# Four groups of head probabilities turned by transfer instead of on TensorE, and the last eight mixer blocks in a new order

## The reference, cut to what matters

```python
def hybrid_mixer(h, mem, positions, ...):
    proj = h @ w_in                       # q, k, v of moba and fox, pool input, memory q, 4 x 1024 gates
    o_a = from_heads(moba_attention(q_a, k_a, v_a))          # 8 heads of 64, causal over 256 rows
    o_b = multiscale_pool(pool_u, pool_mix, pool_scale)
    o_c = from_heads(forgetting_attention(q_c, k_c, v_c, log_f))   # 8 heads of 64, causal, decaying
    o_m = memory_cross_attention(mem_q, mem, ...)            # 4 heads of 128
    branches = jnp.stack([o_a, o_b, o_c, o_m], axis=2)
    y = jnp.einsum('bsnc,ncd->bsnd', branches, w_branch)
    gates = jax.nn.sigmoid(gate_logits.reshape(b, s, N_BRANCH, D_MODEL))
    return jnp.sum(gates * y, axis=2) @ w_out

def softmax_times_values(logits, v):      # the core of each attention
    p = jax.nn.softmax(logits, axis=-1)
    return jnp.einsum('bhqk,bhkd->bhqd', p, v)
```

## Time and profile before

| | |
|---|---|
| median of 3 runs | 1324.23 us (1324.18 to 1324.59) |
| the profiled execution | 1324.54 us, of which its span is 1322.70 us |
| PE busy | 1317.1 us of the span, 6092 matmuls |
| PE's weight loads / DVE / ACT / POOL busy | 1088.3 / 933.0 / 689.6 / 293.1 us |
| granted TensorE clock | 1.00 over the run |
| the chain that ended last | PE 99% |
| in the stretch 334 to 385 us (steps 59 to 66 or so, layer 0) | PE 51.00 of 51 us, DVE 50.13, ACT 30.75, POOL 23.75 |
| in 385 to 436 us | PE 51.00 of 51 us, DVE 38.56, ACT 30.55, POOL 4.19 |

### The profile page before, as it was taken

The page is one execution under the profiler, slowest core; times in us unless marked ns, Lnnn a source line. Parts: engine busy times, 40 slices in busy tenths (PEclk is TensorE's granted clock), DMA queues, the critical chain, the costliest instruction groups (busy, mean ns, idle before and its releaser), DMA issues.

```text
span 1322.7 us, 15761 instructions
## 1 busy us (share of the span) xinstructions
PE 1317.1 (100%) x6092; PEld 1088.3 (82%) x6092; DVE 933.0 (71%) x1174; ACT 689.6 (52%) x956; POOL 293.1 (22%) x280
## 2 busy tenths in 40 slices
PE   9999999999999999999999999999999999999999
PEld 7888888888888888888888888888888878888887
DVE  6666777789987675665475664787999876665653
ACT  5444465554756455444455454556556554645442
POOL 0324312033431002323003230020524110023220
PEclk9999999999999999999999999999999999999999
DMA  9877566567666447777557775555767665577671
GB/s 320 257 216 223 173 230 202 192 179 265 201 178 212 161 149 248 204 225 215 191 191 223 210 228 192 194 165 177 221 223 199 207 195 179 173 225 222 208 215 64
DMA packets 205354, 269.48 MB, mean 204 GB/s; under 512 B 94160, under 2 KB 103904, under 8 KB 205280
## 3 DMA queue, kind: packets, MB, share of 16 engines
q1 hardware_dynamic: 204096, 265.24, 64.9%
q0 software_dynamic: 896, 3.16, 0.7%
q10 hardware_dynamic: 288, 0.07, 0.0%
HBM read 245.37 MB, written 1.06 MB: 186 GB/s over the span
## 4 chain that ended last, share of the span: by engine, by line
PE 99%; DMA 0%; DVE 0%; issue 0%; ACT 0%; SPq 0%; DVEq 0%; ACTq 0%
PE psum L699 24%; PE psum L962 23%; PE psum L726 21%; PE psum L707 12%; PE psum L967 12%; PE psum L920 1%; PE psum L820 1%; PE psum L858 1%; PE psum L924 1%; PE psum L867 1%; PE psum L825 1%; PE psum L654 0%; PE psum L836 0%; PE psum L905 0%; PE psum L861 0%; PE psum L805 0%
## 5 line engine op out<-in xcount | busy, mean ns | idle before, releaser
L1452 DVE TENSOR_TENSOR ring_lo<-raw,ring_hi 128x1024 fp32r<-128x1024 f32 x459 | 598.7, 1318 | 317.1 <-ACT ring_hi L1033 315.5
L1033 ACT ACTIVATE ring_hi<-raw 128x1024 fp32r<-128x1024 f32 x463 | 481.5, 1048 | 555.8 <-PE psum L707 235.5
L699 PE MATMUL psum<-ring_hi,hT 128*128 128x512 f32 x1408 | 348.1, 389 | 1.0 <-DVE ring_hi L1896 1.0
L699 PEld LDWEIGHTS psum<-ring_hi,hT 128*128 128x128 f32 x1408 | 264.2, 188 | 56.0 <-DVE ring_hi L1896 1.2
L962 PE MATMUL psum<-ring_hi,hT 128*128 128x512 f32 x960 | 240.1, 392 | 0.0
L962 PEld LDWEIGHTS psum<-ring_hi,hT 128*128 128x128 f32 x960 | 178.4, 188 | 38.4 <-issue 1.0
L707 PE MATMUL psum<-ring_lo,hT 128*128 128x512 f32 x704 | 188.4, 389 | 0.0
L1340 POOL COPY planes<-gate 128x1024 uint16<-128x1024 uint16 (+1 forms) x48 | 69.0, 1465 | 455.8 <-DVE gate L1526 455.8
L707 PEld LDWEIGHTS psum<-ring_lo,hT 128*128 128x128 f32 x704 | 131.9, 188 | 27.2
L967 PE MATMUL psum<-ring_lo,hT 128*128 128x512 f32 x480 | 128.3, 389 | 0.0
L1350 POOL COPY prodT<-planes_T 128x512 uint16<-128x512 uint16 (+1 forms) x96 | 87.4, 977 | 104.4 <-DMA planes_T<-planes 104.4
(11 more groups left out here) (196 smaller groups left out, 1199.7 us busy)
## 6 DMA issues: line engine op xcount, KB each, us to landing
raw<-in_w_ffn_in SPq DMA_DIRECT2D x78, 1024.0 KB, 5.3
raw<-in_w_in SPq DMA_DIRECT2D x64, 1024.0 KB, 5.5
raw<-in_w_ffn_out SPq DMA_DIRECT2D x44, 1024.0 KB, 5.0
raw<-in_w_branch SPq DMA_DIRECT2D x16, 1024.0 KB, 5.6
raw<-in_w_ffn_in SPq DMA_DIRECT2D x19, 512.0 KB, 4.9
raw<-in_w_mem_kv SPq DMA_DIRECT2D x8, 1024.0 KB, 5.1
raw<-in_w_out SPq DMA_DIRECT2D x8, 1024.0 KB, 5.0
forget<-negc_rows POOLq DMA_DIRECT2D x2, 1024.0 KB, 8.3
```

The source lines that it names most:

```text
L699: pe.matmul(outs[t][:, :], hT[part][:, kc, t * P:(t + 1) * P], w[0][:, kc - first, :], start=kc == 0 and part == 0, stop=False)
L1033: act.activation(unit_out(0, step, k), view, ACT.Copy).then_inc(hi_done.sem, 1)
L1452: dve.tensor_tensor(unit_out(1, step, k), view, unit_out(0, step, k).bitcast(F32), ALU.subtract)\
```

## The change

Groups 3 and 5 join groups 2 and 4: all four head groups are turned by planes, and the PE way (`BY_PE`, the `probsT` stage, its three semaphores) is gone. Group 3's planes are written by ACT at step 63, its transfers are behind the load of step 69 (second home: the memory branch's `vals`), and its `values` move from step 64 END to step 68 MIDDLE. Group 5's planes are written at step 73, its transfers are behind the load of step 78, and its `values` move from step 74 MIDDLE to step 76 MIDDLE. In both branches the blocks come as gate, gate, y, y: after the change the steps are 67/68 gate (0,0), 69/70 gate (0,1), 71 y (0,0), 72 y (0,1), 73/74 gate (2,0), 75/76 gate (2,1), 77 y (2,0), 78 y (2,1). Group 5's scores move from step 71 to step 70 and its exps from 72 to 71. The turn of the first half of z moves from the end of step 77 to the middle of step 78, and DVE adds y (2,0) before the remainder of step 79's second unit.

```diff
     for n in (0, 2):
         for dh in range(2):
             block("gate", (n, dh))
+        for dh in range(2):
             block("y", (n, dh), 1)
...
-_plan("zT", 0, _step_of("gate", (2, 1), 1))
+_plan("zT", 0, _step_of("y", (2, 1)), pe=MIDDLE, act=MIDDLE, dve=START)
...
-BY_DMA, BY_PLANES, BY_PE = (0, 1), (2, 4), (3, 5)
-PLANES_BEHIND = {_step_of("y", (3, 1)): 2, _step_of("gate", (2, 0), 1): 4}
+BY_DMA, BY_PLANES = (0, 1), (2, 3, 4, 5)
+PLANES_BEHIND = {_step_of("y", (3, 1)): 2, _step_of("gate", (0, 1)): 3, _step_of("gate", (2, 0), 1): 4, _step_of("y", (2, 1)): 5}
...
-    (3, _step_of("kc", None, 1), _step_of("gate", (3, 1)), _step_of("gate", (3, 1), 1), _step_of("y", (3, 1))),
-    (4, _step_of("gate", (0, 0)), _step_of("gate", (0, 0), 1), None, _step_of("y", (0, 1))),
-    (5, _step_of("gate", (0, 1), 1), _step_of("y", (0, 1)), _step_of("gate", (2, 0)), _step_of("gate", (2, 0), 1)),
+    (3, _step_of("kc", None, 1), _step_of("gate", (3, 1)), _step_of("gate", (3, 1), 1), _step_of("gate", (0, 0), 1)),
+    (4, _step_of("gate", (0, 0)), _step_of("gate", (0, 0), 1), _step_of("gate", (0, 1)), _step_of("y", (0, 1))),
+    (5, _step_of("gate", (0, 1), 1), _step_of("y", (0, 0)), _step_of("gate", (2, 0)), _step_of("gate", (2, 1), 1)),
...
-                elif stage == "probsT":
-                    pe.wait_ge(probs_ready.sem, probs_ready.at(L, arg + 1))
-                    for j in range(2):
-                        for odd in range(2):
...
-                merged(L, 4)
+                for g in BY_PLANES[1:]:
+                    merged(L, g)
...
+                    summing = (kind, arg) == ("y", (2, 0))
+                    if summing:
+                        serve(L, MIX0 + i, kind, arg, half)
                     ahead(L, MIX0 + i, 1)
                     tasks(L, i, EARLY)
-                    serve(L, MIX0 + i, kind, arg, half, (lambda: lo(L, MIX0 + i + 3, 0)) if kind == "qa" else None)
+                    if not summing:
+                        serve(L, MIX0 + i, kind, arg, half, (lambda: lo(L, MIX0 + i + 3, 0)) if kind == "qa" else None)
```

More of the change, by code:

```diff
@@ L161 @@
     TASKS.setdefault(("DVE", _step_of("vc"), (MIDDLE, EARLY)[t]), []).append(("causal", t))
-_plan("zT", 0, _step_of("gate", (2, 1), 1))
+_plan("zT", 0, _step_of("y", (2, 1)), pe=MIDDLE, act=MIDDLE, dve=START)
 _plan("zT", 1, _step_of("out", 0))
-BY_DMA, BY_PLANES, BY_PE = (0, 1), (2, 4), (3, 5)
-PLANES_BEHIND = {_step_of("y", (3, 1)): 2, _step_of("gate", (2, 0), 1): 4}
+BY_DMA, BY_PLANES = (0, 1), (2, 3, 4, 5)
+PLANES_BEHIND = {_step_of("y", (3, 1)): 2, _step_of("gate", (0, 1)): 3, _step_of("gate", (2, 0), 1): 4, _step_of("y", (2, 1)): 5}
 TURNED_BEHIND = dict(zip([_step_of("ka"), _step_of("gate", (3, 0), 1)], BY_DMA))
-for g, scores, exps, turned, summed in [
+for g, scores, exps, planes, summed in [
     (0, _step_of("y", (1, 0)), _step_of("qa"), None, _step_of("gate", (1, 1), 1)),
     (1, _step_of("gate", (1, 1), 1), _step_of("y", (1, 1)), None, _step_of("qc")),
-    (2, _step_of("gate", (3, 0)), _step_of("gate", (3, 0), 1), None, _step_of("gate", (3, 1), 1)),
-    (3, _step_of("kc", None, 1), _step_of("gate", (3, 1)), _step_of("gate", (3, 1), 1), _step_of("y", (3, 1))),
-    (4, _step_of("gate", (0, 0)), _step_of("gate", (0, 0), 1), None, _step_of("y", (0, 1))),
-    (5, _step_of("gate", (0, 1), 1), _step_of("y", (0, 1)), _step_of("gate", (2, 0)), _step_of("gate", (2, 0), 1)),
+    (2, _step_of("gate", (3, 0)), _step_of("gate", (3, 0), 1), _step_of("y", (3, 0)), _step_of("gate", (3, 1), 1)),
+    (3, _step_of("kc", None, 1), _step_of("gate", (3, 1)), _step_of("gate", (3, 1), 1), _step_of("gate", (0, 0), 1)),
+    (4, _step_of("gate", (0, 0)), _step_of("gate", (0, 0), 1), _step_of("gate", (0, 1)), _step_of("y", (0, 1))),
+    (5, _step_of("gate", (0, 1), 1), _step_of("y", (0, 0)), _step_of("gate", (2, 0)), _step_of("gate", (2, 1), 1)),
 ]:
@@ L181 @@
     if g in BY_PLANES:
[L182 to L185, removed]
+        TASKS.setdefault(("ACT", planes, EARLY), []).append(("planes", g))
+    _plan("values", g, summed, pe=MIDDLE if g in (2, 3, 5) else END, act=MIDDLE if g == 2 else START if g == 5 else EARLY,
           dve=START if g in (1, 2, 5) else EARLY)
@@ L362, in build @@
         head_merged = tally("head_merged", len(BY_PLANES))
-        pT_ps = tally("pT_ps", len(BY_PE))
-        pT_act = tally("pT_act", len(BY_PE))
-        pT_dve = tally("pT_dve", len(BY_PE))
         pv_ready = tally("pv_ready", 6)
@@ L433, in planes_out @@
         def planes_out(g):
-            homes = [kmem[:, :, :], qkT_buf[:, FOX % 2, 1]] if g // 2 == MOBA else [qkT_buf[:, MOBA % 2, i] for i in range(2)]
+            homes = [kmem[:, :, :], vals[:, MEM] if g % 2 else qkT_buf[:, FOX % 2, 1]] if g // 2 == MOBA else [qkT_buf[:, MOBA % 2, i] for i in range(2)]
             return [words.rearrange("p t c -> p (t c)")[:, 0:768].bitcast(U16) for words in homes]
@@ L811, in task @@
                     if arg >= 2:
-                        attended(L, arg - 1 if arg - 1 in BY_PLANES else arg)
+                        attended(L, max(2, arg - 1))
                     if arg:
@@ L841, in task @@
                         pe.wait_ge(pT_merged.sem, pT_merged.at(L, BY_DMA.index(arg) + 1))
-                    elif arg in BY_PLANES:
+                    else:
                         pe.wait_ge(head_merged.sem, head_merged.at(L, BY_PLANES.index(arg) + 1))
[L844 to L847, removed]
+                        pe.wait_ge(max_ready.sem, max_ready.at(L, min(arg + 2, 6)))
                     if arg:
@@ L1217, in task @@
                     last.then_inc(head_planes.sem, 1)
-                elif stage == "probsT":
-                    act.wait_ge(pT_ps.sem, pT_ps.at(L, BY_PE.index(arg) + 1))
-                    act.activation(pT[:, 0, :], bank[4][:, :], ACT.Copy).then_inc(pT_act.sem, 1)
                 elif stage == "pooled":
@@ L1685, in task @@
                             dve.wait_ge(planes_ready.sem, planes_ready.at(L, BY_DMA.index(arg - 1) + 1))
-                        elif arg - 1 in BY_PLANES:
+                        else:
                             dve.wait_ge(head_planes.sem, head_planes.at(L, BY_PLANES.index(arg - 1) + 1))
-                        else:
-                            dve.wait_ge(pT_ps.sem, pT_ps.at(L, BY_PE.index(arg - 1) + 1))
                         if arg // 2 == MOBA:
@@ L1722, in task @@
                     dve.tensor_scalar(negc, csum, -float(HD ** 0.5), None, ALU.mult).then_inc(negc_ready.sem, 1)
[L1723 to L1727, removed]
                 elif stage == "share":
```

## The result

The changed kernel takes 1328.64 us (median of 6 runs, 1327.78 to 1330.84), the kernel before in the same session 1324.48 us (6 runs, 1324.18 to 1324.74): a ratio of 1.0033, 95% interval 1.0023 to 1.0043. It is slower by 4.2 us, where 4.1 were forecast. Its profiled execution took 1328.82 us, with a span of 1327.0.

The account below looks back on a forecast made before the run. PE, busy 1317.1 of 1322.7 us, was taken to bound the kernel, paying every new wait in full. Waits of 4.75 us a layer, 9.5 for two, less 5.4 removed gave +4.1: 1328.3 us, range 1321.8 to 1331.5.

Parts of the forecast that it names:

- The removed work: PE's turning matmuls of groups 3 and 5 go: 1.35 us each, four over two layers, 5.4 us off.
- (a): Gate (2,0) behind y (0,0): PE waits 1.6 us a layer for DVE's addition, delayed by group 4's merge; 0.3 to 2.2.
- (b): Group 5's values, middle of step 76: PE waits 2.2 us a layer for POOL's merging copies; 0.3 to 4.0.
- the two copies near 1.8 us: Sign in group 5's merge: about 6 us, not 4.2, with two of its copies near 1.8 us.
- (c): First half of z, middle of step 78: PE waits 0.35 us a layer behind DVE's addition; 0.1 to 0.5.
- (d): Scores of group 4: PE waits 0.4 us a layer for DVE's scaling of the turned keys; none to 1.2.
- (e): Group 3's values, middle of step 68: PE waits 0.2 us a layer for merge or group 4's maximum; 0 to 0.5.
- the clock stays at 1.00: The clock was granted at 1.00 throughout before, and no change was expected.
- the high ends: All waits at the top of their ranges: 8 us a layer, not likely at once.
- the merges hide (1): POOL's copies not held up at gate (2,0) and group 5's values: 2.8 us waits, both layers, 1321.6 us; chance 0.14.
- half hide (2): Divisions meet only the merge's end, group 5's merge one remainder: 2.45 us a layer, 1323.7 us; chance 0.28.
- Late transfers (3): Group 5's transfers take group 2's 9.1 us, so its values wait 4.0 us: 1331.9 us; chance 0.10.

Follow-up runs that it names:

- y_first: Changed kernel with DVE adding y (0,0) right behind that step's share, before the next step's remainders: 1328.01 us, ratio 1.0020.
- order_again: Second execution, for its trace, of the kernel before with only the new block order, groups 3 and 5 still turned by TensorE: 1327.64 us.
- merge5_twice: Changed kernel with GpSimd's six merging copies of group 5 made twice in each layer: 1340.30 us.
- values4_middle: Changed kernel with group 4's values half a step earlier and group 5's planes one step earlier: 1323.88 us, ratio 0.9996 against the kernel before.
- keys_first: Changed kernel with GpSimd waiting before group 3's merging copies until VectorE has scaled the fox keys: 1328.92 us.

## Why the prediction was right

**The removed work** was 5.4 us: the distances at steps 63 (4.08 to 2.72) and at group 5's turn (4.06 to 2.72) fell by 1.34 to 1.36 us each, in both layers. Right.

**(a)** 1.6 forecast, 1.33 measured, and y_first shows that DVE's addition is what PE waits for. Its two parts were 0.3 bare and 1.3 from group 4's copies. The two divisions of the share took 2.83 us in after, where before they took 1.83, so the copies cost 1.0 and 0.3 is left for the bare chain:

```profile
415.15 2.83 DVE L1709 TENSOR_TENSOR probs<-probs,rden 128x512 f32<-128x512 f32 x2
```

The bare part was right and the copies' part 0.3 too high. In order_again the pair took 2.83 us too and a was the same, so both parts belong to the order: it puts group 4's merge onto the divisions. How the 1.33 divides was only read from rows; no run moved the copies away.

**(b)** 2.2 forecast, 2.06 in layer 0, with the merge at 5.98 us as forecast. The copies begun after PE's end of step 73, slowed by the remainders, are the cause, by merge5_twice (longer by 4.17, wait by 4.15) and values4_middle (begun earlier, no wait). The slowing is in single copies: the first and the fourth, each issued while a remainder ran (437.92 to 439.15, 440.64 to 442.15), took 1.66 and 1.72 us, the other four 0.75 to 0.77. The first two rows are after's, the third is merge5_twice's second six, with no remainder beside them:

```profile
438.11 1.66 POOL L1387 COPY pT<-qkT 128x512 uint16<-128x512 uint16 x1 [21.16 <-DMA qkT<-pT]
441.04 1.72 POOL L1387 COPY pT<-qkT 128x512 uint16<-128x512 uint16 x1
```

```profile
444.55 4.08 POOL L1388 COPY pT<-qkT 128x512 uint16<-128x512 uint16 x6
```

These are the two copies near 1.8 us that the prediction named as its sign. No run moved the remainders themselves.

**(c)** 0.35 against 0.28, **(d)** 0.4 against 0.51 and 0.34, **(e)** 0.2 against 0: right within 0.2 us each. In (d) I had put a low end for an unimpeded scaling at no wait; keys_first still waits 0.23 in layer 0 and not at all in layer 1.

**What failed** is the sentence that the clock stays at 1.00. It fell behind b's wait in layer 1 and gave 1.58 us that no term had. The sum came out right because the other errors point the other way: over both layers a, c, d and e were forecast at 5.1 and came to 4.07, and b's bare wait at 4.4 came to 4.12. That is 1.3 us too much, against 1.6 of clock too little: that they cancel is luck. It is also luck of the runs, since three of the changed kernel's six had a mean clock of 1.000 (1327.78 to 1328.46 us) and three 0.999 or 0.997 (1328.82 to 1330.84). One slip in the ranges changes nothing: the high ends add up to 8.4 us a layer, not 8.

**The rivals.** That the merges hide (1) or half hide (2) fell with the 5.98 us merge. Late transfers (3) fell: the merge began 5.6 us after they were issued at 432.50. What I had not seen is that the change is two changes: the order costs 3.2 us and buys 1.1 at group 3 and room at group 5 that was only estimated, and group 5's planes lose only because they are written after step 73.

## What to carry to other kernels

When one engine is 99% busy, count a change as work removed less every wait added, and measure waits from start to start of a regular group and not by idle time, since the work behind a wait can run at the lower clock. A turn that leaves the busy engine needs its start, not its length, moved: the same 6 us of copies cost 2 to 3.6 us a layer begun at 438.11 and nothing begun at 433.50. Test reordering and offloading apart: the 4.2 us did not show that the order alone cost 3.2 and that group 5's planes gain 2.8 once they start a step earlier.

## What the runs showed of the hardware that was not expected

- After idle stretches of 1.98 to 1.99 us of PE the granted clock fell to 0.50 in some executions and layers and not in others (after and keys_first: layer 1 only; y_first: both), at 1.5 to 1.6 us each time. After 6.13 us it fell in both layers, at 1.97 and 2.70 us. After 1.25 us it never fell in the traces here. What decides at 1.98 us stays open. The changed kernel's runs spread over 3.1 us and sort by their mean clock, where before's in the same session spread over 0.6.
- DVE's scaling of one 128x1024 SBUF operand went from 0.75 to 1.25 us beside POOL's copies, and DVE's remainders there from 1.2 to 1.73. POOL's copies in turn went from 0.76 to as much as 1.7.
- The values of group 1 in layer 1, which wait for one transposing transfer and POOL's copies behind it, cost PE 0.07 to 1.6 us beyond their usual distance from one execution to the next, in kernels that don't differ there.
